# A recurrent layer on one core: the first matrix work of the next head pair is issued inside a pair's steps, which use two PSUM banks

## The reference

```
def step(s, inp):                      # per head, s is 64 x 64
    r_t, w_t, k_t, v_t, kk_t, a_t = inp
    sa = einsum('bhvk,bhk->bhv', s, -kk_t)
    s = s * w_t + sa * (kk_t * a_t) + v_t * k_t
    return s, einsum('bhvk,bhk->bhv', s, r_t)
o = o_forward + o_backward             # then normed per head,
o = normed(o) * lnx_w + lnx_b + bonus  # bonus = sum(r * k * r_k) * v
out = (o * g) @ wo
```

## Time and profile before

| | |
|---|---|
| median of 3 runs | 1683.1 us (1678.05 to 1689.67) |
| the profiled execution's own time | 1680.41 us |
| its span in the profile | 1678.6 us |
| granted clock of TensorE, mean | 0.942 |
| TensorE matmuls, busy | 1494.4 us, 89% of the span |
| weight loads | 957.6 us, 57% |
| VectorE | 613.7 us, 37% |
| ScalarE | 526.4 us, 31% |
| GpSimd | 265.2 us, 16% |
| recurrence, first own product to last step | 374.9 us |

### The profile page before, as it was taken

The page is one execution under the profiler, slowest core; times in us unless marked ns, Lnnn a source line. Parts: engine busy times, 40 slices in busy tenths (PEclk is TensorE's granted clock), DMA queues, the critical chain, the costliest instruction groups (busy, mean ns, idle before and its releaser), DMA issues. The chain is left out here.

```text
span 1678.6 us, 41121 instructions
## 1 busy us (share of the span) xinstructions
PE 1494.4 (89%) x17678; PEld 957.6 (57%) x17678; DVE 613.7 (37%) x1520; ACT 526.4 (31%) x1202; POOL 265.2 (16%) x260
## 2 busy tenths in 40 slices
PE   3998878878999999959998898888988779999997
PEld 1554556445555555535557777777774455555554
DVE  2003673243111111541306776666661521111116
ACT  2113553232111111220136665665441321111122
POOL 0000031002000001010045454455500110000010
PEclk8999889898999999979999999899998989999999
DMA  9324556737799999612200000000003369999992
GB/s 390 122 101 158 222 207 248 286 116 310 295 379 381 370 376 383 266 50 100 100 26 4 6 6 5 6 6 6 4 6 151 127 275 354 380 367 379 379 384 95
DMA packets 54036, 328.33 MB, mean 196 GB/s; under 512 B 6646, under 2 KB 10038, under 8 KB 18712
## 3 DMA queue, kind: packets, MB, share of 16 engines
q1 hardware_dynamic: 43632, 290.07, 44.8%
q0 software_dynamic: 5184, 18.88, 2.8%
q10 hardware_dynamic: 5096, 17.58, 2.7%
HBM read 304.35 MB, written 22.16 MB: 195 GB/s over the span
## 5 line engine op out<-in xcount | busy, mean ns | idle before, releaser
L1398 PE MATMUL ps<-ring,arena 128*64 128x256 f32 x2048 | 243.2, 385 | 6.3 <-ACT arena L1513 5.2
L1398 PEld LDWEIGHTS ps<-ring,arena 128*64 128x64 f32 x2048 | 141.9, 137 | 97.0 <-issue 36.0
L298 PE MATMUL ps<-HT,ring 128*128 128x384 f32 x544 | 180.9, 496 | 14.2 <-PEq L367 8.2
L298 PEld LDWEIGHTS ps<-HT,ring 128*128 128x128 f32 x544 | 105.5, 194 | 89.6 <-issue 20.1
L1408 PE MATMUL ps<-ring,arena 128*32 128x128 f32 x4096 | 133.8, 278 | 0.0
L1602 DVE TENSOR_TENSOR arena<-arena,ps 64x256 f32<-64x256 f32 (+1 forms) x128 | 40.6, 357 | 252.5 <-ACT arena L1519 252.5
L1434 PE MATMUL ps<-ring,arena 128*64 128x512 f32 x512 | 129.8, 605 | 0.0
L1408 PEld LDWEIGHTS ps<-ring,arena 128*32 128x32 f32 x4096 | 107.7, 111 | 27.0 <-issue 25.4
L1518 ACT ACTIVATE arena<-ps 64x256 f32<-64x256 f32 x64 | 24.2, 377 | 309.6 <-PE ps L1398 309.6
L298 PE MATMUL ps<-arena,ring 128*128 128x384 f32 x256 | 85.3, 497 | 18.8 <-DVEq L2051 18.8
L1526 ACT ACTIVATE arena<-ps 32x256 f32<-32x256 f32 x128 | 47.9, 374 | 160.3 <-PE ps L1434 159.2
(11 more groups left out here) (357 smaller groups left out, 2280.4 us busy)
## 6 DMA issues: line engine op xcount, KB each, us to landing
ring<-wstream SPq DMA_DIRECT2D x272, 1024.0 KB, 7.4
moe_rows<-arena ACTq DMA_DIRECT2D x28, 384.0 KB, 6.9
arena<-moe_tokens POOLq DMA_DIRECT2D x12, 512.0 KB, 15.2
moe_rows<-arena ACTq DMA_DIRECT2D x4, 512.0 KB
consts<-cst ACTq DMA_DIRECT2D x1, 1655.0 KB, 17.2
XT<-xT ACTq DMA_DIRECT2D x1, 1536.0 KB, 11.2
yT<-HT SPq DMA_DIRECT2D x3, 384.0 KB, 3.2
arena<-wa SPq DMA_DIRECT2D x1, 1024.0 KB, 4.8
```

Source lines behind the costliest of these rows:

```text
L298: mm = pe.matmul(bank(m % 8), w[:, k, m % 2 * P:m % 2 * P + P], rhs[:, k, :], start=k == 0, stop=k == KC - 1)
L1398: mm = pe.matmul(bank(h, 256)[HD * x:HD * x + HD], TOKE[:, k, 0:MANY], w[:, kk, x, :], start=k == 0, stop=k == KC - 1)
```

## The change

`matrices_*` becomes `inverse_*`, which begins with the right products of level 1. Own products, block masks, first sums, first transposes and left products of level 1 of pair c+1 (`nx`) are issued in the steps of pair c; for pair 0 alone they stand ahead of the loop. The steps use bank 3 for right-hand side and growth (`STATE_BANK`) and bank 7 for solved values and both outputs (`SOLVED_BANK`), since banks 0 to 2 now receive the next pair's matrices; left and right products share banks 4 and 5, low-rank products use 3 and 7. The key norm of pair c+2 (`j`) is made in step 2. GpSimd makes the key times the root first, and the normed output and the bonus factors behind the operands, with a semaphore of their own. Value rows move to levels 4 and 5, operand rows and bonus product to level 5. SP loads a pair's states behind the last output of the pair before.

```diff
-        LEFT_BANKS, RIGHT_BANKS, SIDE = (3, 7), (4, 5), 6
-        LORA_BANKS, FIRST_BANKS, FIRST_SIDE = (4, 5, 7, SIDE), (3, 4, 5, 6), 0
+        LEFT_BANKS, RIGHT_BANKS, SIDE = (4, 5), (4, 5), 6
+        STATE_BANK, SOLVED_BANK = 3, 7
+        LORA_BANKS, FIRST_BANKS, FIRST_SIDE = (3, 7, 3, 7), (3, 4, 5, 6), 0
         def prep_pool(pool, j, b, c):
+            pool.wait_ge(s_krr, j + 1)
+            pool_o(pool.tensor_tensor(KK, KK, KK2, ALU.mult))
             pool.wait_ge(s_kd, j + 1)
             pool_o.inc(pool.tensor_tensor(dt(KDF), dt(KDF), kb, ALU.mult))
-            pool.wait_ge(s_krr, j + 1)
-            pool_o(pool.tensor_tensor(KK, KK, KK2, ALU.mult))
             pool_o.inc(pool.tensor_tensor(dt(KKAF), dt(KKAF), kkb, ALU.mult))
-            if b is not None:
-                out_pool(pool, b)
...
+            pool_o.wait()
+            pool.sem_inc(s_op, 1)
+            if b is not None:
+                out_pool(pool, b)
...
-            pool.sem_inc(s_op, 1)
+            pool.sem_inc(s_kkb, 1)
             @block.sync
-                    sp.wait_ge(s_af, c + 1)
+                    if c:
+                        sp.wait_ge(s_out, c * 4)
+            def inverse_act(act, c, j, b):
+                for g, h in enumerate(halves):
+                    act.activation(AB[h, g], AR[h, :, :, 0, :], ACT.Copy)
+                    last = act.activation(RM[h, g], AR[h, :, :, 1, :], ACT.Copy)
+                    if g == 0 and j is not None:
+                        sigmoids_act(act, j, LORA_BANKS, (0, 1))
+                last.then_inc(s_cc, 1)
+                if b is not None:
+                    squares_act(act, b)
+                if j is not None:
+                    sigmoids_act(act, j, LORA_BANKS, (2, 3))
+                    act.wait_ge(s_kkb, c + 1)
+                    factors_act(act, j)
+                    exps_act(act, j)
+                if b is not None:
+                    scale_act(act, b)
...
             def steps_act(act, c, nx, j):
...
                     act.wait_ge(s_oz, c * 4 + (s + 1))
-                    act.activation(OS[:, x:x + w], lanes_of(2, w, slice(0, P)), ACT.Copy).then_inc(s_ozc, 1)
+                    act.wait_ge(s_sv, c * 4 + (s + 1))
+                    act.activation(OS[:, x:x + w], lanes_of(SOLVED_BANK, w, slice(0, P), 256), ACT.Copy).then_inc(s_ozc, 1)
+                    if s == 1 and j is not None:
+                        act.wait_ge(s_op, j)
+                        inputs_act(act, j)
+                    if s == 2 and j is not None:
+                        root_act(act, j)
+                if nx is not None:
+                    raw_act(act, nx)
             def steps_dve(dve, c, nx):
...
+                        if s == 2:
+                            blocks_dve(dve, nx, 1)
+                        if s == 3:
+                            first_sums_dve(dve, nx, 1)
                     dve.wait_ge(s_so, c * 4 + (s + 1))
...
+                        if s == 2:
+                            first_sums_dve(dve, nx, 0)
+                        if s == 3:
+                            first_level_dve(dve, 1)
...
                     dve.sem_inc(s_os, 1)
+                        if s == 1:
+                            blocks_dve(dve, nx, 0)
+                        if s == 2:
+                            first_level_dve(dve, 0)
+            def inverse_pe(pe, c, j, b):
+                if j is not None:
+                    if b is not None:
+                        pe.wait_ge(s_os, b * 4 + 4)
+                    lora_pe(pe, j, 0, LORA_BANKS[0])
+                    lora_pe(pe, j, 1, LORA_BANKS[1])
+                right_pe(pe, c, 1, 0)
+                right_pe(pe, c, 1, 1)
...
+                left_pe(pe, c, 2, 0)
+                pe.wait_ge(s_m1, c + 1)
+                crossed_pe(pe, c, 0)
+                left_pe(pe, c, 2, 1)
+                crossed_pe(pe, c, 1)
+                right_pe(pe, c, 2, 0)
+                if j is not None:
+                    pe.wait_ge(s_sg, j * 4 + 2)
+                    lora_pe(pe, j, 2, LORA_BANKS[2])
+                    lora_pe(pe, j, 3, LORA_BANKS[3])
+                right_pe(pe, c, 2, 1)
...
+                operand_rows_pe(pe, c, 0)
+                right_pe(pe, c, 5, 0)
+                operand_rows_pe(pe, c, 1)
+                right_pe(pe, c, 5, 1)
+                operand_rows_pe(pe, c, 2)
+                pe.wait_ge(s_vr, c * 3 + 3)
+                pe.wait_ge(s_kkb, c + 1)
+                pe.matmul(bank(SIDE), heads, KKB, start=True, stop=True).then_inc(s_bo, 1)
             def steps_pe(pe, c, nx, j):
...
                     if s:
-                        pe.wait_ge(s_ozc, c * 4 + s)
+                        pe.wait_ge(s_os, c * 4 + s)
...
                     mm.then_inc(s_so, 1)
+                    if nx is not None:
+                        if s == 1:
+                            own_pe(pe, nx, NCH, 2 * NCH)
+                        if s == 3:
+                            left_pe(pe, nx, 1, 0)
+                    if s == 2 and j is not None:
+                        pe.wait_ge(s_bon, c + 1)
+                        norm_pe(pe, j)
...
-                    if s:
-                        pe.wait_ge(s_os, c * 4 + s)
+                    pe.wait_ge(s_ozc, c * 4 + (s + 1))
...
                     mm.then_inc(s_out, 1)
+                    if nx is not None:
+                        if s == 0:
+                            pe.wait_ge(s_op, nx + 1)
+                            own_pe(pe, nx, 0, NCH)
+                        if s == 3:
+                            left_pe(pe, nx, 1, 1)
```

More of the change, by code:

```diff
@@ new lines, in crossed_pe, with value_rows_pe @@
+            def crossed_pe(pe, c, half):
+                for d, n in by_d[half]:
+                    x = (d * NCH + n) * P
+                    for g, h in enumerate(halves):
+                        mm = pe.matmul(ps[halves[1 - g], x:x + P], KB[h, d, n, 1 - g], AR[h, d, n], start=True, stop=True)
+                mm.then_inc(s_ma, 1)
+            def value_rows_pe(pe, c, x):
+                order = [n for s in range(4) for a, d, n in lanes_at(s)]
+                for y in range(4):
+                    n = order[4 * x + y]
+                    mm = pe.transpose(bank(SIDE, P, P * y)[0:HD], of_pair(VT, c)[:, CH * n:CH * n + CH], ident)
+                mm.then_inc(s_rt, 1)
@@ new lines, in operand_rows_pe, with each, left_pe @@
+            def operand_rows_pe(pe, c, x):
+                for y in range(4):
+                    mm = pe.transpose(bank(x, P, P * y), KBE[:, 4 * x + y], ident)
+                mm.then_inc(s_kt, 1)
+            def each(pe, o, left, right, d):
+                for n in range(NCH):
+                    for h in halves:
+                        mm = pe.matmul(bank(o, 32, 32 * n)[h], dn(left)[h, d, n], right[h, d, n], start=True, stop=True)
+                return mm
+            def left_pe(pe, c, n, d):
+                pe.wait_ge(s_inv, c * NINV + (2 * n - 1 + d))
+                if n < NLEV:
+                    mm = each(pe, LEFT_BANKS[d], AF, DC, d)
+                else:
+                    for m in range(NCH):
+                        for g in range(2):
+                            k, i = HD * g + 32 * d, HD * g + 32 * (1 - d)
+                            mm = pe.matmul(bank(LEFT_BANKS[d], 32, 32 * m)[i:i + 32],
+                                           dn(ATF)[k:k + 32, d, m, 32 * (1 - d):32 * (1 - d) + 32],
+                                           DC[k:k + 32, d, m], start=True, stop=True)
+                mm.then_inc(s_ll, 1)
@@ new lines, in right_pe @@
+            def right_pe(pe, c, n, d):
+                pe.wait_ge(s_ls, c * NLL + (2 * n - 1 + d))
+                if n < NLEV:
+                    mm = each(pe, RIGHT_BANKS[d], PF, DTC, d)
+                else:
+                    for m in range(NCH):
+                        for g in range(2):
+                            k, i = HD * g + 32 * d, HD * g + 32 * (1 - d)
+                            mm = pe.matmul(bank(RIGHT_BANKS[d], 32, 32 * m)[k:k + 32], dn(PF)[i:i + 32, d, m, 0:32],
+                                           DTC[i:i + 32, d, m], start=True, stop=True)
+                mm.then_inc(s_lr, 1)
```

336 lines of the change are left out of this document (147 added, 189 removed).

## The result

| | before | after |
|---|---|---|
| median | 1681.8 us (1678.05 to 1689.67, 4 runs) | 1728.35 us (1721.05 to 1729.77, 4 runs) |
| profiled execution, its span | 1680.41, 1678.6 us | 1727.24, 1725.5 us |
| mean granted clock | 0.942 | 0.908 |
| the loop | 374.9 us | 423.3 us |

The ratio is 1.026, its 95% interval 1.021 to 1.031. Slower, and outside the predicted range. One execution of the first experiment's ten, 3705.89 us, was in a slow state and stands in no ratio. The loop gained 48.4 us, the whole span 46.9: all of the loss lies in the recurrence.

What follows compares the result with a forecast made beforehand. The prediction took the loop to be bound by a chain on the core, not a full engine. At full clock +1.8 us, with -10.6 from the clock, gave -8.8 on 1680.4: 1672 us, range 1657 to 1688.

Steps and rivals of the forecast that it cites:

- What bounds the kernel: Recurrent loop: time set on the core by a chain; TensorE mostly waits in a pair's 8.85 us front.
- The walk: Prediction's wait-by-wait estimate of a pair at full clock: front -8.85, steps +4.35, inverse +3.85, balance -0.65 us.
- The steps: A pair's four recurrence steps, now 15.3 us: gain 4.35 us from the next pair's first-level work placed in them.
- The inverse: A pair's inverse, now 20.95 us, level by level: gains 3.85 us, mostly in levels 2 and 5.
- The meeting with GpSimd: VectorE's identity sum in the steps waits for GpSimd's root product: 0.87 us in six pairs, +5.2 us.
- The scan's row: Earlier trace: VectorE's scan beside a GpSimd product of 1.81 us took 2.56 instead of 0.92; basis for the 0.87.
- The sign that the prediction set: Identity sum beside GpSimd's product would take 1.2 us or more in one of two calls of a pair.
- The sum at full clock: Whole loop without clock effects: -3.4 us from the reordering, +5.2 from waiting on GpSimd, together +1.8 us.
- The clock: Loop's 14.1 us lost to the lower clock: three quarters come back as the thin front stretch goes, -10.6 us.
- (B): Rival, loop: clock no better, falls only move; +1.8 us, 1682 us; chance 0.18.
- (A): Rival, loop: no meeting with GpSimd and the clock stays up; -17.5 us, 1663 us; chance 0.27.
- (C): Rival, step 0: TensorE waits for GpSimd's operands, so slower; 1694 us at 6 us late; chance 0.08.

Runs made afterwards that it cites:

- the first experiment: The changed kernel with filler matmuls, result never read, in TensorE's gaps of steps 1 to 3 and levels 3 and 4: 1676.6 us, ratio 0.997.
- the small filler: The changed kernel with filler in all pairs, one filler pair in step 3 instead of three: 1663.4 us with GpSimd's root product behind its key product, 1670.7 ahead.

## Why the prediction was wrong

**What bounds the kernel** holds: the loop is a chain on the core itself, and all the change is in it. But the 8.85 us of a pair's front are not a time "in which TensorE mostly waits":

```profile
930.02:938.87 8.85, 7.77 (x113) 5.40 (x109) 6.91 (x20) 6.28 (x10) 0.00 (x0) 1.00 0.03 9
```

It is busy for 7.77 of them, with the low-rank products in most of the gaps. The walk had these products again in the inverse, so its sum doesn't suffer; its picture of what was taken out does.

**The steps** (20.5 us forecast with the meeting, 19.65 without): 20.39 at full clock. Right in sum, though some terms miss and partly cancel: the meeting is 0.53 and not 0.87, so the rest came to 19.9.

**The inverse** (24.8 forecast): in the profile of the small filler it runs from 1020.88 to 1045.07, 24.2 us, filler included. Levels 3, 4 and 5 were each within 0.35 us in after; level 2, whole at full clock in the small filler's profile, took 5.8 where 6.3 was forecast.

**The meeting with GpSimd**: right in kind and place (once a pair, six pairs; the one in the first front was missed), too large in size. The scan's row lent nearly the whole product; here the sum began 0.32 us into the product of 1.00, when 0.68 were left of it, and lost 0.53. The Trainium skill (SBUF — State Buffer, "SBUF: two separate sides") states a lock held for a whole instruction; the scan of the earlier trace rows and this sum agree with it in the main: the sum ended 0.21 us behind GpSimd's product, 0.15 sooner than if all its 0.36 had come behind it. The sign that the prediction set, 1.2 us or more, was thereby missed too.

**The sum at full clock** was +1.8 us, from 360.8 to 362.6. Measured without falls: 363.73 for the changed order with its meeting against 361.67 for the order before, +2.1. Both hold some filler, most of which lies in waits (level 3 takes 5.5 us with its four pairs and 5.05 without), so each is an upper bound for its order. The difference of the two is no such bound: against the 360.8 of before without filler it is 2.9. As far as these loops show it, the change would thus have cost 2 to 3 us even with the clock up, and gives 1 to 2 in the loop once GpSimd's product is moved (359.85).

**The clock** is the step that failed. "I take three quarters: -10.6" was to leave 3.5 us of the 14.1. By the same filler loops the clock cost at least 374.9 - 361.67 = 13.2 us before and 423.3 - 363.73 = 59.6 us after: +46.4 instead of -10.6. That difference of 57 us is the error, which is 56.4 by the medians (1728.35 for 1672). 14 falls at 59.6 us are 4.3 us each; a pair with two takes 54.1 where one without takes 45.1, 4.5 each.

Where the reasoning went astray can be named from the text. It took the thin stretch out and asked what follows there; of the stretches that receive the work it said "some more if the longer steps 2 and 3 bring falls of their own", and gave this no price. It also spoke of "1 fall of 8" at the end of the steps, where the trace of before has seven falls. Two windows of before, from the start of step 2 to the end of the steps and over the own products behind them, then its level 3, and one of after, from the start of step 2 to the last left product:

```profile
970.12:975.12 5.00, 3.46 (x72) 2.77 (x74) 2.43 (x8) 2.17 (x9) 0.00 (x0) 1.00 0.05 15
975.12:978.00 2.88, 2.88 (x56) 2.71 (x53) 1.29 (x7) 2.24 (x3) 0.00 (x0) 1.00 0.02 6
...
947.05:951.75 4.70, 4.34 (x105) 3.75 (x104) 4.17 (x9) 2.62 (x6) 3.80 (x5) 1.00 0.02 3
```

```profile
1094.71:1102.25 7.54, 5.29 (x99) 3.90 (x99) 6.58 (x18) 3.83 (x11) 1.11 (x2) 1.00 0.03 9
```

Before, TensorE was busy 3.46 of 5.0 us, and then fully for the 2.9 us of the own products. After, it is busy 5.29 of 7.5 us: about the same share, but half as long again, and what follows is the rest of the first level, since the own products have gone to steps 0 and 1. Seven of the fourteen falls begin there or with that left product. Six more (one in the first pair) begin behind level 3, of which the prediction's part on the clock says nothing: the length of the level it had to 0.1 us, but it didn't ask what the level would look like without its transposes and with a longer wait at its end: TensorE busy 4.34 of 4.70 us before, 4.07 of 5.05 after. Work that was taken out of a stretch counted as a gain only.

These windows show what changed, not a measure that sorts the stretches. The one that the prediction named as the cause of the falls before was busy 4.81 of 5.30 us, more than the steps that no fall followed; only filler, put in or left out, showed which stretches matter.

The Trainium skill (TensorE: Matmul & The Clock Gate, "What's actually happening") was cited for the whole 14.1 to come back, because the lack of activity would end. The filler runs agree with the rule: with matmuls added and nothing taken away, the clock of the changed loop went from 0.78 to 0.97 and 1.00. It cuts both ways, though: the stretches that the change left thinner fell under it as well.

**The rivals.** (B), that falls only move, was nearest and stopped at no gain. (A) needed the clock to stay up. (C) did not occur: no wait for GpSimd in step 0, and the side on which slower lay was a different one. The chance of 0.08 for slower was far too small for a change that touched the density of every stretch of a chain that already fell seven times.

**What stays open.** Which of the pieces that were moved brings the fall behind level 3 was asked once, and new waits spoiled the answer. Also open is what makes a stretch thin enough, since the busy share doesn't show it and level 3 was followed by a fall in six pairs of eight, and why the falls of after last 10 to 17 us where three of before ended after 3.4; a dense block behind the steps shortened those of the steps, and none was tried for the inverse.

## What to carry to other kernels

Before moving work out of one place in a chain of short matmuls, write down for every stretch that it leaves and enters what TensorE does there and what follows, and give further falls of the clock a price; a walk of waits right to about 0.5 us a part was worth little beside fourteen falls of 4.3 us. Try a new order at once with some matmuls of filler in its waits: one to three pairs a place were enough here, and they separate what the order is worth (45.1 us a pair of heads, or 44.6 with GpSimd's product moved, against 45.4 for the order before with filler and 45.1 without) from what the clock makes of it. And read the busy share beside the granted clock: nines over sixes and sevens are not a full engine.

## What the runs showed of the hardware

- The busy share rises as the work slows. Level 4 of after, 104 records, once at full clock and once with the fall in it: busy 4.34 of 4.69 us, then 5.60 of 5.60.

```profile
1072.91:1077.60 4.69, 4.34 (x104) 3.75 (x104) 4.07 (x9) 2.01 (x5) 4.61 (x8) 1.00 0.01 3
1175.54:1181.14 5.60, 5.60 (x104) 4.77 (x104) 4.01 (x8) 2.00 (x5) 5.52 (x8) 0.72 0.01 3
```

- More matmuls made the program faster: 336 records more, 51 us less in the loop.
- Six pairs of filler right behind the thin stretch did not keep the clock up (1734.6 us); filler inside it did (1710.0).
- The same stretch, alike to 0.01 us, was followed by a fall in one pair and not in another.
- VectorE's sum of two SBUF operands, begun while GpSimd's product runs, loses at most what is left of the product: 0.53 us when 0.68 were left, 0.67 when 0.82 were left; the scan of the earlier trace rows lost 1.64 of 1.75.
